# Delta net stage: gate products behind the spread, neighbour passes taken apart, first modulation products later

## The reference, cut to what matters

```python
def delta_chunked(q, k, v, beta, g, s0):
    ...
    gcum = jnp.cumsum(to_chunks(g[..., None])[..., 0], axis=-1)
    decay = jnp.exp(jnp.where(causal, gcum[..., :, None] - gcum[..., None, :], -jnp.inf))
    k_beta = kc * bc[..., None]
    m = jnp.where(strict, jnp.einsum('nbhid,nbhjd->nbhij', k_beta, kc) * decay, 0.0)
    rhs = jnp.concatenate([vc * bc[..., None], k_beta * jnp.exp(gcum)[..., None]], axis=-1)
    sol = lax.linalg.triangular_solve(eye + m, rhs, left_side=True, lower=True, unit_diagonal=True)
    u, w = sol[..., :dv], sol[..., dv:]
    attn = jnp.einsum('nbhid,nbhjd->nbhij', qc, kc) * decay
    q_dec = qc * jnp.exp(gcum)[..., None]
    ...
    def step(S, xs):
        u_i, w_i, q_i, k_i, attn_i, gl = xs
        v_new = u_i - jnp.einsum('bhck,bhkv->bhcv', w_i, S)
        o = jnp.einsum('bhck,bhkv->bhcv', q_i, S) + jnp.einsum('bhij,bhjv->bhiv', attn_i, v_new)
        S = S * jnp.exp(gl)[..., None, None] + jnp.einsum('bhck,bhcv->bhkv', k_i, v_new)
        return S, o
...
for l in range(DEPTH):
    mod_x = (jax.nn.silu(c) @ w_mod[l] + b_mod[l])[:, None, :]
    sh1, sc1, g1, sh2, sc2, g2 = jnp.split(mod_x, 6, axis=-1)
    hx = rms_norm(xs, norm_mix_g[l]) * (1 + sc1) + sh1
    ...
```

## Time and profile before

| | |
|---|---|
| time of the profiled execution | 1393.43 us |
| its span | 1391.3 us |
| PE busy | 1324.6 us, 95% |
| DVE busy | 888.4 us, 64% |
| ACT busy | 697.5 us, 50% |
| POOL busy | 254.1 us, 18% |
| chain that ended last, by engine | PE 75%, DVE 9%, ACT 5%, issue 5%, POOL 4%, DMA 1% |
| granted TensorE clock, whole span | 0.982 |

### The profile page before, as it was taken

One profiled execution on the slowest core, in us unless ns is written; L12 is line 12 of the kernel. 1 busy time (PEld: TensorE's weight loads), 2 busy tenths in 40 slices (PEclk: granted clock), 3 DMA queues, 4 the chain that ended last, 5 costly groups with the idle time before them and its releaser, 6 DMA issues.

```text
span 1391.3 us, 27306 instructions
## 1 busy us (share of the span) xinstructions
PE 1324.6 (95%) x10946; PEld 1242.3 (89%) x10946; DVE 888.4 (64%) x1413; ACT 697.5 (50%) x1123; POOL 254.1 (18%) x240
## 2 busy tenths in 40 slices
PE   6999999999688888999999999999999999999998
PEld 3899999987477777799999999999999988999998
DVE  3755889886366676653377756566645666876663
ACT  4468888878244444432354311243225656664553
POOL 2000224210245656541200000000011000200002
PEclk8999999999799999999999999999999999999999
DMA  9632222222310000022346556565522420557662
GB/s 325 190 85 84 84 84 81 87 85 68 107 60 32 31 32 32 32 91 92 130 153 201 190 182 191 183 202 184 165 91 93 136 77 16 168 168 223 185 199 90
DMA packets 138029, 170.67 MB, mean 123 GB/s; under 512 B 10912, under 2 KB 121760, under 8 KB 137920
## 3 DMA queue, kind: packets, MB, share of 16 engines
q1 hardware_dynamic: 137312, 168.94, 38.7%
q0 software_dynamic: 608, 0.19, 0.1%
HBM read 168.06 MB, written 1.05 MB: 122 GB/s over the span
## 4 chain that ended last, share of the span: by engine, by line
PE 75%; DVE 9%; ACT 5%; issue 5%; POOL 4%; DMA 1%; SPq 0%; DVEq 0%; ACTq 0%; POOLq 0%
PE bank L2682 55%; PE bank L2690 4%; DVE w_lo L1722 2%; PE bank L3086 2%; POOL d_t L821 1%; PE bank L3095 1%; DVE qkv L1808 1%; ACT w_hi L921 1%; PE bank L2608 1%; DMA first_w<-in_w_mod 1%; PE bank L3352 1%; PE bank L3375 1%; PE bank L3065 1%; POOL qkv L786 1%; PE bank L2945 1%
## 5 line engine op out<-in xcount | busy, mean ns | idle before, releaser
L1722 DVE TENSOR_TENSOR w_lo<-raw,w_hi 128x1024 fp32r<-128x1024 f32 x212 | 264.4, 1248 | 297.0 <-ACT w_hi L921 296.7
L921 ACT ACTIVATE w_hi<-raw 128x1024 fp32r<-128x1024 f32 x212 | 223.4, 1055 | 374.4 <-PE bank L2682 372.6
L2682 PE MATMUL bank<-h_hi,w_hi 128*128 128x256 f32 x1472 | 300.4, 282 | 5.5 <-DVE w_lo L1722 3.0
L2682 PE MATMUL bank<-h_hi,w_lo 128*128 128x256 f32 x1472 | 293.8, 278 | 0.0
L2682 PE MATMUL bank<-h_lo,w_hi 128*128 128x256 f32 x1472 | 288.3, 278 | 0.0
L2682 PEld LDWEIGHTS bank<-h_hi,w_hi 128*128 128x128 f32 x1472 | 225.9, 188 | 15.2 <-issue 10.2
L2682 PEld LDWEIGHTS bank<-h_hi,w_lo 128*128 128x128 f32 x1472 | 225.6, 188 | 0.0
L2682 PEld LDWEIGHTS bank<-h_lo,w_hi 128*128 128x128 f32 x1472 | 222.5, 188 | 0.3 <-DVE h_lo L2003 0.2
L2682 PE MATMUL bank<-hid_hi,w_hi 128*128 128x256 f32 x768 | 171.9, 278 | 0.0
L2682 PE MATMUL bank<-hid_lo,w_hi 128*128 128x256 f32 x768 | 170.8, 277 | 0.0
L2682 PE MATMUL bank<-hid_hi,w_lo 128*128 128x256 f32 x768 | 170.8, 277 | 0.0
(11 more groups left out here) (376 smaller groups left out, 2497.0 us busy)
## 6 DMA issues: line engine op xcount, KB each, us to landing
raw<-in_mlp_w SPq DMA_DIRECT2D x128, 512.0 KB, 3.7
late_w<-in_w_mod SPq DMA_DIRECT2D x56, 512.0 KB, 4.4
raw<-in_even_w_in SPq DMA_DIRECT2D x48, 512.0 KB, 3.7
raw<-in_w_mod SPq DMA_DIRECT2D x24, 512.0 KB, 4.3
first_w<-in_w_mod SPq DMA_DIRECT2D x16, 512.0 KB, 11.2
raw<-in_even_w_out SPq DMA_DIRECT2D x16, 512.0 KB, 3.5
raw<-in_attn_w_qkv SPq DMA_DIRECT2D x16, 512.0 KB, 3.5
raw<-in_attn_w_o SPq DMA_DIRECT2D x8, 512.0 KB, 3.4
```

What stands on the lines that cost most here:

```text
L921: act.activation(stored(w_hi, j, four), raw[:, j % RAW], ACT.Copy).then_inc(hi_ready, 1)
L1722: dve.tensor_tensor(stored(w_lo, j, four), raw[:, j % RAW], stored(w_hi, j, four).bitcast(F32), ALU.subtract).then_inc(split_done, 1)
L2682: return pe.matmul(bank[2 * pair + t][:, c - n0:c - n0 + CTX], w_[:, k, t * P:(t + 1) * P], x_[:, c:c + CTX], start=(kk == 0 and first and ...
```

## The change

Five things move; no arithmetic is added or taken away.

- POOL: the gate products of direction 1 (`log_gates(q + 2, 1)`) went ahead of `spread(q + 1)`; now both directions stand behind the spread and `decayed_values`.
- VectorE: `neighbours` was one run of three passes ahead of `reduced(q, 1, 0)`; now the first pass stands behind `masked(q, 1, 1)`, the other two behind `reduced(q, 1, 1)`. The first part of `local(q + 1)` goes ahead of `rest_of_v(q - 1, 1)`.
- TensorE: the neighbour product goes ahead of the third part's fillers and of `second_product(q, 2, 0)`. ScalarE: its copies go ahead of `flipped(q, 1, 1)`, and the second row exponential ahead of `betas(q + 2)`.
- The eight modulation units of step 0 stand at parts 3 to 6 of the step, not at 0 to 5, and the split of the w_out unit is earlier on ScalarE and VectorE.
- Before the stage, `neighbours(0)` on ScalarE and `local(0)` on VectorE are at place w = 2 of the last z body, not 3.

```diff
...
 BY_PE = 5 * MOD_BATCH
-FILLERS = {0: {0: 1, 1: 2, 2: 1, 3: 2, 4: 1, 5: 1}, 7: {2: 2, 4: 2}}
+FILLERS = {0: {3: 2, 4: 2, 5: 2, 6: 2}, 7: {2: 2, 4: 2}}
 LATE = 56
...
                     lru_half(1)
-                if q + 2 < STEPS:
-                    log_gates(q + 2, 1)
                 if prep:
...
                 if q + 2 < STEPS:
+                    log_gates(q + 2, 1)
                     log_gates(q + 2, 0)
...
                     decay(0)
-                if b == LRU_TILES + 1 and w == 3:
+                if b == LRU_TILES + 1 and w == 2:
                     neighbours(0)
...
             flipped(0, -1, 1)
+            split_hi(SEG["out"]["unit"] + 1, 1)
             betas(1)
...
                     squares(q - 2)
-                if q == 0:
-                    split_hi(SEG["out"]["unit"] + 1, 1)
                 flipped(q, 1, 0)
                 gathered(q, 1, 1)
-                flipped(q, 1, 1)
                 if prep:
                     neighbours(q + 1)
+                flipped(q, 1, 1)
                 gathered(q, 2, 0)
...
                 flipped(q, 2, 1)
+                if prep:
+                    rows(q + 1, 0)
                 if q + 2 < STEPS:
...
                 if prep:
-                    rows(q + 1, 0)
                     gathered(q + 1, -1, 0)
...
                     system(0)
-                    neighbours(0)
-                if b == LRU_TILES + 1 and w == 3:
+                    for part in range(3):
+                        neighbours(0, part)
+                if b == LRU_TILES + 1 and w == 2:
                     local(0)
...
-            def neighbours(q):
-                dve.wait_ge(v_n, q + 1)
-                link(dve.tensor_tensor(d_b[:, :, :], d_n[q % 2][:, :, :], C("local").unsqueeze(1).to_broadcast([P, 4, P]), ALU.mult))
-                link(dve.tensor_reduce(n_rows, d_b[:, :, :].rearrange("p i (b c) -> p i c b", c=LOCAL), mybir.AxisListType.X, ALU.add))
-                dve.tensor_tensor(flat(d_b[:, 0:2]).rearrange("p (i r c) -> p i r c", i=4, r=LOCAL),
-                                  n_rows.unsqueeze(2).to_broadcast([P, 4, LOCAL, LOCAL]),
-                                  place_of.unsqueeze(1).unsqueeze(3).to_broadcast([P, 4, LOCAL, LOCAL]), ALU.mult).then_inc(v_near, 1)
+            def neighbours(q, part):
+                if part == 0:
+                    dve.wait_ge(v_n, q + 1)
+                    link(dve.tensor_tensor(d_b[:, :, :], d_n[q % 2][:, :, :], C("local").unsqueeze(1).to_broadcast([P, 4, P]), ALU.mult))
+                if part == 1:
+                    link(dve.tensor_reduce(n_rows, d_b[:, :, :].rearrange("p i (b c) -> p i c b", c=LOCAL), mybir.AxisListType.X, ALU.add))
+                if part == 2:
+                    dve.tensor_tensor(flat(d_b[:, 0:2]).rearrange("p (i r c) -> p i r c", i=4, r=LOCAL),
+                                      n_rows.unsqueeze(2).to_broadcast([P, 4, LOCAL, LOCAL]),
+                                      place_of.unsqueeze(1).unsqueeze(3).to_broadcast([P, 4, LOCAL, LOCAL]), ALU.mult).then_inc(v_near, 1)
...
                 masked(q, 0, 1)
+                if q == 0:
+                    split_lo(SEG["out"]["unit"] + 1, 1)
                 if tail:
...
                     values(q - 1, 0)
-                if prep:
-                    neighbours(q + 1)
                 reduced(q, 1, 0)
                 masked(q, 1, 1)
-                if q == 0:
-                    split_lo(SEG["out"]["unit"] + 1, 1)
+                if prep:
+                    neighbours(q + 1, 0)
                 scores(q)
...
                 reduced(q, 1, 1)
+                if prep:
+                    neighbours(q + 1, 1)
+                    neighbours(q + 1, 2)
                 if flip_turn(q):
...
                 masked(q, 2, 1)
+                if prep:
+                    local(q + 1, LOCAL - 1, 4)
                 if tail:
                     rest_of_v(q - 1, 1)
-                if prep:
-                    local(q + 1, LOCAL - 1, 4)
                 masked(q, 3, 0)
...
                     state(t, 0)
+                if prep:
+                    neighbours(q + 1)
                 mod_filler(mods_in(q, 3))
...
                 flip(q, 1, 1)
-                if prep:
-                    neighbours(q + 1)
                 if tail:
```

## The result

The changed kernel takes 1359.78 us (median of three, 1356.94 to 1361.57) against 1393.41; the ratio is 0.9753, with an interval from 0.9719 to 0.9787. The forecast was 1361.7. They add up to 36.5 us, where the medians differ by 33.6: the profiled execution is the fastest of its three. A second set of the changed kernel (e14), run beside the last experiments, gave 1360.30 and 0.9775 [0.9748, 0.9802]; 1359 to 1361 and 0.974 to 0.977 were expected of it.

What follows compares the result with a forecast made beforehand. Dense matmul on TensorE bounds the kernel nearly everywhere, except the DeltaNet stage, where small engines hold it. 1.5 + 11 + 5.7 + 8.0 + 5.5 = 31.7 us, from 1393.4 to 1361.7; 8 in 10 for 1353 to 1374.

Steps and rivals of the forecast that it cites:

- ahead of step 0: Before step 0's first product: earlier local(0) brings it forward, though it then waits for normalisations; 1.5 us, bounds 0 and 3.5.
- step 0: Step 0: the w_mod transfer wait goes and the neighbour product comes 12.9 us earlier; 11 us gained, bounds 7 and 13.
- middle of steps 1 to 6: Mid-step: the wait for reduced goes, a smaller one comes at the neighbour product; 5.7 us, bounds 0 and 9.
- gate products behind the spread: End of local, steps 1 to 5: two small VectorE operations fall back to 0.19 us; 8.0 us, bounds 5 and 8.
- clock of steps 1 to 6: Shorter waits at steps' ends let four steps keep full clock, at 1.36 us each; 5.5 us, bounds 0 and 8.
- partly beside VectorE's `local`: Step 0, neighbour product to next step's first product, 9.95 us: eight units (4 us) lie there, partly beside local.
- the first of them is at most 1 us late, which the wait for the spread hides: Step 0's last four units: slots come from the first four, and a transfer takes 3.86 us from issue to landing.
- rival that step 0 was not held by the transfer: Step 0: units queue for slots or the POOL and VectorE chain ends unchanged; only 5 of 11 us, 1368; chance 0.12.
- rival of the moved wait: Mid-step: moved passes stretch beside POOL and the product comes as before; middle and clock terms 0, 1373; chance 0.13.
- so I cost it at nothing, at the edge: POOL: four products delay masked_scores, whose end falls near where the betas' multiplication starts anyway; cost 0.
- rival of the late POOL: Four products stretch and masked_scores ends 1 us after the exponential; 5 us lost in five steps, 1367; chance 0.08.
- The row exponential: Step's end: 1.63 us of blendings leave the path to tokens; alone no gain, a cover for the earlier local.

Runs made afterwards that it cites:

- e14: Second set of the changed kernel, nothing altered, run beside the last experiments against the kernel before; 1360.30 us, ratio 0.9775.
- e8: Changed kernel with local(0) and the copies of neighbours(0) back at place w = 3 of the last z body; 1361.92 us, ratio 0.9792.
- e3: Changed kernel with the three neighbour passes whole and ahead of reduced again, product and copies at their old places too; 1370.02 us, ratio 0.9825.
- e7: Kernel before with direction 1's gate products behind the spread and the second row exponential ahead of the blendings; 1381.13 us, ratio 0.9888.
- e2: Changed kernel with the gate products of direction 1 ahead of the spread again, on POOL; 1372.08 us, ratio 0.9843.
- e1: Changed kernel with step 0's eight modulation units and the two splits of the w_out unit back at their old places; 1366.75 us, ratio 0.9807.
- e5: Kernel before with only step 0's eight modulation units at parts 3 to 6 and the two splits early; 1382.14 us, ratio 0.9897.
- e6: Kernel before with only the gate products of direction 1 moved behind the spread; 1384.35 us, ratio 0.9916.
- e4: Changed kernel with the blendings of the betas ahead of the second row exponential again, on ScalarE; 1367.17 us, ratio 0.9799.
- e13: Changed kernel with the blendings ahead of the second row exponential again and one modulation unit of steps 1 to 6 ahead of the tokens; 1359.73 us, ratio 0.9760.

## Why the prediction was right, point by point

The forecast was 1361.7, against 1359.78 measured and 1356.94 in the profiled execution. Its five terms:

| term | forecast us | measured us | from |
|---|---|---|---|
| ahead of step 0 | 1.5 | 1.8 | e8 |
| step 0 | 11 | 11.1; 9.7 in the second set | stretches |
| middle of steps 1 to 6 | 5.7 | 7.7 (7.8 by e3) | waiting, after against e7 |
| gate products behind the spread | 8.0 | 6.4 (7.0 by e2) | waiting, e7 against before |
| clock of steps 1 to 6 | 5.5 | 8.6 | busy time, after against before |
| sum | 31.7 | 35.6 | |

*Ahead of step 0.* As forecast: the first product now waits for the normalisations.

*Step 0.* The sum came out and its inside did not, so that it came out is in part luck. The neighbour product came 15.50 us after the first one, not at the forecast's 17.51 (367.05 less 349.54): the forecast had taken over the pace of before, where the first four records took 1.20 us for 0.68 now. In the second set, whose step 0 began at half clock, it was 16.7 us. The piece behind it took 13.10 us (361.50 to 374.60), not 9.95, and two steps failed there. One is the piece's own work, "partly beside VectorE's `local`": TensorE is busy for 11.80 of the 13.10 us, and `local` began 4.7 us after the product where it had been 1.3, because `reduced` stands ahead of it and waits for a second product behind the two slow units:

```profile
365.29 0.42 DVE L2307 TENSOR_TENSOR d_t<-d_t,bank 128x256 f32<-128x256 f32 x1 [3.85 <-PE bank L3101]
```

So the spread ended at 373.16, 11.7 us after the product. The other is "the first of them is at most 1 us late, which the wait for the spread hides": it took 3.86 us for a transfer where with four under way it is 6.08. The last two units waited 0.64 and 0.66 us, and no wait for the spread hid it; TensorE came to the first product 1.4 us after the spread. Of the 11.1 us, 6.4 are waiting and 4.7 the clock; the 1.2 taken off for a clock that might fall had the wrong sign, since the step went from 0.80 to 0.94. It is the part that scatters: its clock was 0.94 and 0.89 in two executions of one kernel. The rival that step 0 was not held by the transfer is out by e1 and e5; the waiting for slots that it named came, at 1.3 us.

*The middle.* In step 3 the forecast held within 0.2 us: 0.94 of wait at the product for its 1.1. Step 1 gave 1.7 us for 1.2 (e3, less the 0.72), and the even steps were mis-sized, 1.04 to 1.20 us for 0.7: their product has no wait above 0.3 us left, where the forecast kept some. The rival of the moved wait was half right in its mechanism, since the first pass did stretch from 0.68 to 1.40 us beside POOL; the other two took 1.08 and 0.67, and there was room for that.

*The gate products.* The stretched operations fell to 0.2 us as forecast. The step "so I cost it at nothing, at the edge" failed: ScalarE waits 1.22 us for masked_scores, and TensorE 0.46 for ScalarE, in steps 3 and 5. It is the rival of the late POOL at a fifth of its price, 0.9 us for 5. It runs over the exponential that overwrites masked_scores' input, not over the betas' multiplication, which the forecast looked at.

*The row exponential.* A cover, as forecast: without it the gate products give 3.3 us of waiting (e6), with it 6.4 (e7), and taken from the changed kernel it costs 3.1 us of waiting and 4.7 of clock (e4).

*The clock.* The forecast had four steps at 1.36 us. Five of the six had been below 1.00 and all five came to it: busy time fell by 3.0 us in step 1, by 1.1 to 1.7 each in steps 2, 3, 4 and 6, and not in step 5, which had 1.00 already. The price of 1.36 was read from lengths (30.38 less 29.02); 0.43 of it is waiting (5.12 less 4.69), and the clock's part only 0.93 (25.26 less 24.33). The direction held, and that and the middle make most of what the sum lacks. How much of the 8.6 us belongs to the shorter waits is not settled: e5 has 4.2 of it with the waits of steps 1 to 6 unchanged. What the runs do show is that no step from 2 to 6 whose waits were 1.5 us or shorter lost the clock, in 41 cases. To the 35.6 come 1.8 us ahead of the stage that belong to no part, less 0.9 behind it: 36.5, the difference of the profiled times.

## What to carry to other kernels

Split each stretch into waiting and busy time before costing a reordering: here 13 of 36 us came back as clock (4.7 in step 0 and 8.6 in steps 1 to 6), and no row of waits shows them. Where several waits end a step, ask of each which one stands just behind it; a move that removes the last one gains only the distance to the next (e6), and a second move can free the rest (e7). A slot's transfer is to be costed with as many in flight as the new order puts there, and an operation moved behind another on an engine with slack is to be followed to whoever overwrites its operands.

## What the runs showed of the hardware

*Where the clock falls.* In steps 2 to 6 of all fourteen executions profiled (70 steps), no step whose waits at its start and inside it were 1.5 us or shorter ran below 1.00 (41 of 41). Of the 29 with a wait of 1.8 us or longer, 17 ran at 0.93 to 0.95, each with 1.1 to 1.7 us more busy time than the same step at 1.00, and 12 kept 1.00 or 0.99. The same wait of 2.03 us stood before slow and before full steps, even in one kernel, so what decides among those stays open. What is shown is that two waits of 0.7 us, or one of 1.45, cost no clock here, and one of 2.0 often does (e4 against e13).

*POOL beside VectorE.* An operation of 0.2 us on VectorE took 0.90 to 1.03 us where it began soon after a POOL product of 1.04 us, and ended within 0.1 us of it, in every step of before and of e2 in which the two met. One that began 0.19 us before the product's end took 0.24; without a product it was 0.2. These operations read both inputs from SBUF. Those that read a bank of PSUM were not touched: `reduced` took 0.41 to 0.42 us in steps 0 to 6 of before, thirty times beside a POOL instruction and twenty-five times not. The price of an overlap was what was left of POOL's instruction, however small VectorE's, so a chain of small dependent operations is the worst place for one.
